# A hybrid decoder step: the level products of a gated recurrence, read with both heads' keys over all 128 rows

## The reference

```python
def step(S, inp):                      # 4 heads, dk = dv = 64
    qi, bi, ki, vi = inp               # bi: running sum of log forget gates
    diff = bi[:, :, :, None, :] - bi[:, :, None, :, :]
    decay = jnp.exp(jnp.where(causal[:, :, None], diff, NEG_BIG))
    att = jnp.einsum('bhtc,bhsc,bhtsc->bhts', qi, ki, decay)
    o = jnp.einsum('bhts,bhsv->bhtv', att, vi) + jnp.einsum('bhtc,bhcv->bhtv', qi * jnp.exp(bi), S)
```

## Time and profile before

| | us |
|---|---|
| median of 3 runs (827.66 to 829.39) | 829.32 |
| the profiled execution, time | 829.25 |
| its span, first to last instruction | 827.5 |
| PE busy | 816.1 (99%) |
| DVE busy | 570.0 (69%) |
| ACT busy | 436.8 (53%) |
| POOL busy | 264.2 (32%) |

### The profile page before, as it was taken

How to read it: one execution, slowest core, us unless ns; L and a number is a source line. 1 busy time by engine, 2 the same in 40 slices (tenths; PEclk the granted TensorE clock), 3 DMA queues, 4 the chain that set the end, 5 groups by cost and what they waited for, 6 DMA issues and landing times.

```text
span 827.5 us, 18120 instructions
## 1 busy us (share of the span) xinstructions
PE 816.1 (99%) x7016; PEld 801.4 (97%) x7016; DVE 570.0 (69%) x768; ACT 436.8 (53%) x621; POOL 264.2 (32%) x230
## 2 busy tenths in 40 slices
PE   9999999999999999999999999999999999999995
PEld 8999999999999999999999999999999999999995
DVE  7778787676877666554576688957787776645553
ACT  6553376645557665434353634774555666643442
POOL 4585282036710000121147825801565000001220
PEclk9999999999999999999999999999999999999999
DMA  9896859767657778776659968887665876776751
GB/s 314 235 319 256 301 162 324 237 227 269 218 179 253 240 241 306 248 262 226 205 164 247 312 234 278 241 259 256 232 237 179 260 247 221 260 280 234 250 203 52
DMA packets 171035, 200.00 MB, mean 242 GB/s; under 512 B 19680, under 2 KB 168496, under 8 KB 169648
## 3 DMA queue, kind: packets, MB, share of 16 engines
q1 hardware_dynamic: 169584, 197.02, 72.4%
q10 hardware_dynamic: 1392, 2.15, 0.7%
HBM read 191.25 MB, written 51.90 MB: 294 GB/s over the span
## 4 chain that ended last, share of the span: by engine, by line
PE 95%; DVE 3%; DMA 0%; ACT 0%; issue 0%; DVEq 0%; ACTq 0%
PE main L644 28%; PE main L645 28%; PE main L646 27%; PE small L694 2%; PE small L660 1%; PE small L646 1%; PE small L645 1%; PE small L644 1%; DVE w_lo L1189 1%; PE small L705 1%; DVE h_lo L1205 0%; DMA raw<-in_w_in 0%; PE small L798 0%; PE small L853 0%; PE small L722 0%; PE main L615 0%
## 5 line engine op out<-in xcount | busy, mean ns | idle before, releaser
L954 ACT ACTIVATE w_hi<-raw 128x1024 fp32r<-128x1024 f32 (+1 forms) x256 | 266.2, 1041 | 247.9 <-PE main L646 186.9
L1189 DVE TENSOR_TENSOR w_lo<-raw,w_hi 128x1024 fp32r<-128x1024 f32 (+1 forms) x256 | 337.3, 1318 | 64.6 <-ACT w_hi L954 60.6
L644 PE MATMUL main<-h_hi,w_hi 128*128 128x264 f32 x1264 | 365.6, 289 | 0.9 <-DVE w_lo L1189 0.8
L645 PE MATMUL main<-h_lo,w_hi 128*128 128x264 f32 x1264 | 358.8, 284 | 0.0
L646 PE MATMUL main<-h_hi,w_lo 128*128 128x264 f32 x1264 | 358.6, 284 | 0.0
L644 PEld LDWEIGHTS main<-h_hi,w_hi 128*128 128x128 f32 x1264 | 238.7, 189 | 5.9 <-DVE w_lo L1189 1.7
L645 PEld LDWEIGHTS main<-h_lo,w_hi 128*128 128x128 f32 x1264 | 239.0, 189 | 0.2
L646 PEld LDWEIGHTS main<-h_hi,w_lo 128*128 128x128 f32 x1264 | 237.6, 188 | 0.0
L644 PE MATMUL main<-a_hi,w_hi 128*128 128x264 f32 x512 | 145.3, 284 | 0.0
L645 PE MATMUL main<-a_lo,w_hi 128*128 128x264 f32 x512 | 145.0, 283 | 0.0
L646 PE MATMUL main<-a_hi,w_lo 128*128 128x264 f32 x512 | 145.0, 283 | 0.0
(11 more groups left out here) (222 smaller groups left out, 1030.0 us busy)
## 6 DMA issues: line engine op xcount, KB each, us to landing
raw<-in_w_in SPq DMA_DIRECT2D x48, 1024.0 KB, 5.8
raw<-in_w_up SPq DMA_DIRECT2D x32, 1024.0 KB, 5.3
raw<-in_w_down SPq DMA_DIRECT2D x32, 1024.0 KB, 5.2
out_kvs<-in_cache SPq DMA_DIRECT2D x48, 512.0 KB
out_kvs<-in_cache SPq DMA_DIRECT2D x32, 496.0 KB
raw<-in_w_o SPq DMA_DIRECT2D x8, 1024.0 KB, 5.3
raw<-in_w_br SPq DMA_DIRECT2D x8, 768.0 KB, 5.1
gates<-q_scratch SPq DMA_DIRECT2D x4, 768.0 KB, 7.2
```

Of the source, the lines that this page charges most:

```text
L644: pe.matmul(out[:, 0:TOK], wh, rh, start=start and k == 0, stop=False)
L645: pe.matmul(out[:, 0:TOK], wh, rl, start=False, stop=False)
L954: act.activation(w_hi[:, slot(l, u), 0:k, :], raw_of(u, k), ACT.Copy).then_inc(w_hi_ready, 1)
L1189: dve.tensor_tensor(w_lo[:, slot(l, u), 0:k, :], raw_of(u, k), w_hi[:, slot(l, u), 0:k, :].bitcast(F32), ALU.subtract).then_inc(w_lo_ready, 1)
```

## The change

- **Level products.** The queries are laid out in `q_bd` as head 0's rows with the rest zero, then head 1's rows with the rest zero (POOL clears it, ACT copies twice 64 rows, behind the `w_hi` split of unit 8, `q_bd_ready`). `q_lv` then holds both heads' padded late queries, so one matmul over 128 rows with 2 x 64 query columns serves both heads: 4 matmuls at levels 1 to 7 into one bank, 4 of 256 columns at level 0, 2 of 256 at level 8. Level 1 reads `kg` itself as its keys, so POOL makes no `k_lv` there. DVE's masked copies are one of 512 elements a level instead of two of 256.
- **Start of layer 0.** `unit_lo_last` also serves units 6 and 7; `w_lo` of unit 6 is made ahead of `bounds`, that of unit 7 behind it and ahead of the decays. ACT issues the first weight piece ahead of the small gain load.

```diff
@@ -73,7 +73,8 @@
 TURNS = (
     ["norm1"]
     + ["values T", "sample values T"]
-    + [f"level {i} {h}" for i in range(9) for h in range(2)]
+    + ["level 0 0", "level 0 1"]
+    + [f"level {i}" for i in range(1, 9)]
     + ["recurrence", "decayed keys T", "state"]
     + ["sample q T", "sample kv T 0", "sample kv T 1"]
     + ["scores 0 0", "scores 1 0", "scores 0 1", "scores 1 1", "scores 0 2", "scores 1 2"]
...
@@ -206,6 +207,10 @@
         swapped_qk = gates[:, 4:10, :]
         q_rows = gates[:, 12:24, :].rearrange("p a t -> p (a t)")[:, 0:SAMPLES * NG * P].rearrange(
             "p (b g c) -> p b g c", b=SAMPLES, g=NG)
+
+        q_bd = v_cache[:, :, :, :].rearrange("p b g c -> p (b g c)")[:, 0:4 * PROMPT].rearrange(
+            "p (h a t) -> p h a t", h=2, a=2)
+        final_k = q_lv[:, 1, :, :, :].rearrange("p h a c -> p (h a c)").rearrange("p (a t) -> p a t", a=2)
 
         ident = consts[:, K_ID:K_ID + P]
         ones = consts[:, K_ONE:K_ONE + P]
...
@@ -662,38 +668,31 @@
 
             def level(l, i):
 
-                if i:
-                    pe.wait_ge(level_ready, l * 8 + i)
-                else:
+                if i == 0:
                     pe.wait_ge(kg_ready, l + 1)
-                    z_ready(pe, l, CT_CQ + 1)
-
-                def operands(hp, h):
-                    rows = slice(h * HD, (h + 1) * HD)
-                    if i:
-                        return k_lv[rows, i % 2, hp, :], q_lv[rows, i % 2, hp, :]
-                    return kg[rows, hp, 0:PROMPT], z[rows, CT_CQ + hp, 0:PROMPT]
-
-                def queries(qq, tb):
-
-                    if not i:
-                        return qq[:, tb * P:tb * P + P]
-                    return qq[:, tb * P:tb * P + P].rearrange("p (n s t) -> p n s t", s=2, t=LEVELS[i - 1])[:, :, 1, :]
-                w = HALF if i else P
-                early = P - LEVELS[i - 1] if 0 < i < 8 else P
-                banks = [use_bank(pe, l, f"level {i} {h}") for h in range(2)]
+                    pe.wait_ge(q_bd_ready, l * 2 + 2)
+                    for hp in range(2):
+                        bank = use_bank(pe, l, f"level 0 {hp}")
+                        for tb in range(2):
+                            ts = slice(tb * P, tb * P + P)
+                            mm = pe.matmul(bank[:, tb * 2 * P:(tb + 1) * 2 * P], kg[:, hp, ts], q_bd[:, :, hp, ts],
+                                           start=True, stop=True)
+                        done(mm, f"level 0 {hp}")
+                    return
+                pe.wait_ge(level_ready, l * 8 + i)
+                bank = use_bank(pe, l, f"level {i}")
                 for hp in range(2):
-                    for tb in range(2 if i < 8 else 1):
-                        for h in range(2):
-                            kk, qq = operands(hp, h)
-                            if i == 8:
-                                out, kk, qq = banks[h][:, hp * P:hp * P + P], kk[:, 0:P], qq[:, P:2 * P]
-                            else:
-                                c = (hp * 2 + tb) * w
-                                out, kk, qq = banks[h][0:early, c:c + w], kk[:, tb * P:tb * P + early], queries(qq, tb)
-                            mm = pe.matmul(out, kk, qq, start=True, stop=True)
-                            if hp == 1 and (i == 8 or tb == 1):
-                                done(mm, f"level {i} {h}")
+                    if i == 8:
+                        mm = pe.matmul(bank[:, hp * 2 * P:(hp + 1) * 2 * P], k_lv[:, 0, hp, 0:P], q_lv[:, 0, :, hp, :],
+                                       start=True, stop=True)
+                        continue
+                    early = P - LEVELS[i - 1]
+                    for tb in range(2):
+                        keys = kg[:, hp, :] if i == 1 else k_lv[:, i % 2, hp, :]
+                        c = (hp * 2 + tb) * P
+                        mm = pe.matmul(bank[0:early, c:c + P], keys[:, tb * P:tb * P + early],
+                                       q_lv[:, i % 2, :, hp, tb * HALF:(tb + 1) * HALF], start=True, stop=True)
+                done(mm, f"level {i}")
 
             def scores(l, j, gs):
 
...
@@ -868,9 +867,10 @@
                 for u, (kind, n) in enumerate(UNIT_KINDS):
                     if l == 0 and u < 4:
                         continue
-                    if l == 0 and u < 6:
+                    if l == 0 and u < 8:
                         pe.wait_ge(out_taken, u + 1)
                         unit_lo_last(u, main[u % 4]).then_inc(w_used, 1)
+                        between(l, n)
                         continue
                     pe.wait_ge(w_lo_ready, l * UNITS + u + 5)
                     if kind == "in":
...
@@ -994,6 +994,13 @@
                     step(act.activation(kg[:, :, :], z[:, CT_CF:CT_CF + 2, :], ACT.Sigmoid, scale=-1.0))
                     act.activation(z[:, CT_CF:CT_CF + 2, :], z[:, CT_CF:CT_CF + 2, :], ACT.Sigmoid)\
                        .then_inc(sigmoids, 1)
+                if u == 5:
+                    z_ready(act, l, CT_CQ + 1)
+                    act.wait_ge(q_zeroed, l + 1)
+                    for h in range(2):
+                        rows = slice(h * HD, (h + 1) * HD)
+                        act.activation(q_bd[rows, h, :, :], z[rows, CT_CQ:CT_CQ + 2, 0:PROMPT], ACT.Copy)\
+                           .then_inc(q_bd_ready, 1)
                 if u == 8:
                     z_ready(act, l, CT_CO + 1)
                     act.activation(o_c[:, :, :], z[:, CT_CO:CT_CO + 2, :], ACT.Sigmoid).then_inc(sigmoids, 1)
...
@@ -1090,8 +1096,9 @@
             def square(k):
                 act.activation(square_of(k), x[:, k, :], ACT.Square).then_inc(squared, 1)
 
+            act.dma_start(piece_raw(0), piece_source(0)).then_inc(piece_landed[0], 16)
             act.dma_start(cur[:, C_G1:C_G1 + KT], io["gain0"]).then_inc(gain_in, 16)
-            for i in range(3):
+            for i in range(1, 3):
                 act.dma_start(piece_raw(i), piece_source(i)).then_inc(piece_landed[i], 16)
             act.wait_ge(setup_done, 1)
...
@@ -1269,23 +1276,24 @@
                     if i == 0:
                         dve.wait_ge(levels_in, 16)
                         dve.wait_ge(att_clear, l + 1)
-                    for h in range(2):
-                        name = f"level {i} {h}"
+                    for hp in range(1 if i else 2):
+                        name = f"level {i}" if i else f"level 0 {hp}"
                         bank = take(dve, l, name)
                         wait_ends(dve)
                         if i:
                             half = LEVELS[i - 1]
                             early, n, c = P - half, HALF // half, P + (i - 1) * HALF
-                            dst = att[0:early, h, :, :].rearrange("p a (n s t) -> p a n s t", s=2, t=half)[:, :, :, 1, :]
+                            dst = att[0:early, :, :, :].rearrange("p a h (n s t) -> p (a h) n s t", s=2, t=half)[:, :, :, 1, :]
                             mask = levels[0:early, c:c + HALF].rearrange("p (n t) -> p n t", n=n)
-                            src = bank[0:early, 0:4 * HALF].rearrange("p (a n t) -> p a n t", a=4, n=n)
-                            mask = mask.unsqueeze(1).to_broadcast([early, 4, n, half])
+                            src = bank[0:early, :].rearrange("p (a n t) -> p a n t", a=8, n=n)
+                            mask = mask.unsqueeze(1).to_broadcast([early, 8, n, half])
                         else:
-                            dst, mask = att[:, h, :, :], levels[:, 0:P].unsqueeze(1).to_broadcast([P, 4, P])
+                            dst = att[:, hp * 2:hp * 2 + 2, :, :].rearrange("p a h c -> p (a h) c")
+                            mask = levels[:, 0:P].unsqueeze(1).to_broadcast([P, 4, P])
                             src = bank[:, :].rearrange("p (a c) -> p a c", a=4)
                         ins = dve.copy_predicated(dst, mask.bitcast(U32), src)
                         ins.then_inc(masked, 1)
-                        dve.wait_ge(masked, l * 16 + 2 * i + h + 1)
+                        dve.wait_ge(masked, l * 9 + (i + 2 if i else hp + 1))
                         dve.sem_inc(bank_taken[TURN[name] % 4], 1)
 
                 def mask_scores(j):
...
@@ -1367,10 +1375,11 @@
                         dve.wait_ge(state_s_ready, l + 1)
                     evacuate(l, u)
                     if u == 3:
+                        split_lo(l, at + 3)
                         if l == 0:
                             bounds()
                             new_params()
-                        split_lo(l, at + 3)
+                            split_lo(l, at + 4)
 
                         dve.wait_ge(sigmoids, 2 * l + 1)
                         for hp in range(2):
...
@@ -1491,7 +1500,7 @@
                         dve.wait_ge(y_hi_ready, 3 * l + 3)
                         dve.tensor_tensor(y_lo[:, 0, :], y_a[:, :], y_hi[:, 0, :].bitcast(F32), ALU.subtract)\
                            .then_inc(y_ready, 1)
```

(20 more changed lines are left out.)

28 lines of the change are left out of this document (14 added, 14 removed).

## The result

| | before | changed |
|---|---|---|
| median of 4 runs each | 828.54 | 833.77 (832.98 to 834.67) |
| the profiled execution, time / span | 829.25 / 827.5 | 833.25 / 831.5 |

The ratio is 1.0064 (95% interval 1.0045 to 1.0082): slower, and 0.5 us above the forecast. Both kernels' times come in steps of 1.6 to 1.7 us (before: 827.7 or 829.3). A step is one drop of PE's granted clock to half for 3.41 us, told of at the end. The two profiled executions have one each and lie 4.0 us apart; the medians lie 5.2 apart, since the runs of the kernel before have none or one and those of the changed kernel one or two.

What follows compares the result with a forecast made beforehand. PE, busy 816.1 of 827.5 us, was taken to bound the kernel, with POOL feeding it. 829.25 + 1.65 (level 8) + 2.4 (unit 20) = 833.3; own range 831.2 to 835.5, 8 in 10 827.0 to 836.5.

Steps and rivals of the forecast that it cites:

- the two level terms: Start of level 8 in each layer: PE waits for POOL, +1.0 in layer 0 and +0.65 in layer 1.
- the unit 20 terms: Unit 20 in both layers: PE waits for a DVE split delayed by POOL's later work, +1.2 a layer, +2.4.
- Waits of units 6 and 7, -1.35: Start of layer 0: PE's two waits for `w_lo` go, saving 1.35 us.
- First weight piece earlier, -0.2: Start of layer 0: first weight piece lands up to 0.43 earlier, of which the ACT chain uses 0.2.
- PE's level stages: PE at levels: 0.87 each at levels 1 to 7, level 0 +0.6, level 8 unchanged; -1.1 a layer if PE sets pace.
- The query product, +0.69 a level: POOL at the levels: doubling to 512 elements adds 0.69 a product, making POOL's cycle 4.68 against PE's 3.78.
- Level 8, +1.0 in layer 0 and +0.65 in layer 1: POOL's operands come late, so PE starts level 8 at 67.7 in layer 0 and 472.1 in layer 1.
- The gains of start and PE are spent in this wait: Layer 0: POOL sets level 8's start, 1.0 later than before, so earlier savings at start and PE's levels are lost.
- Unit 20, +1.2 a layer: POOL work pushed behind level 8 locks out DVE's rotary products and splits; PE waits at unit 20, +2.4 in all.
- POOL keeps up: Rival at the levels: query product grows 0.3 or less or splits fit better, no level late; 825.5, chance 0.16.
- PE's stages get dearer: Rival at PE's levels: no edge saved, overlap of two heads' rows lost, +0.5 a layer; 833.8 or 828.7, chance 0.10.

Runs made afterwards that it cites:

- e3: Changed kernel with POOL's query product cut to 256 elements, head 1's half of the padded queries left zero; median 827.20, ratio 0.9988.
- e5: Changed kernel with gain load first and ACT copying the queries into the pads, POOL multiplying 256 elements a level; median 824.69, ratio 0.9960.
- e7: Changed kernel with gain load first and the start part undone, so the level products alone; median 834.81, ratio 1.0075.
- e1: Changed kernel with the small gain load issued ahead of the first weight piece again; median 832.53, ratio 1.0046.
- e4: Changed kernel with DVE's splits of units 19 and 20 moved ahead of its rotary products; median 828.78, ratio 1.0006.
- e6: e5 with e4's edit, the splits of units 19 and 20 ahead of the rotary products; median 824.67, ratio 0.9954.
- e11: Changed kernel with the one-column products divided, half of them moved behind unit 25; runs 831.53 to 832.00.
- e8: e6 with the one-column products divided, half of them moved behind unit 25; runs 825.24 to 825.65.
- e10: e7 with the one-column products divided, half of them moved behind unit 25; runs 831.79 to 832.50.
- e12: Changed kernel with gain load first, ACT making pads, level 0 unpadded, splits of units 19 and 20 before rotary products, one-column products divided; median 824.70, ratio 0.9958.

## Why the prediction was right, and where it was not

The sign, the total (833.3 for 833.77) and the mechanism hold: POOL's doubled query product makes PE wait at levels 6 to 8 and, through DVE, at unit 20; e3 removes the product's second half and both waits. That the total is as close as it is, is luck: errors of its terms cancel. Against the forecast the gain load adds 1.0 at level 8, the rest of the two level terms is 1.9 too large, and the unit 20 terms are 0.7 too small. The forecast start of level 8 in layer 1, 472.1, was met by chance too (472.37): the forecast had left layer 0's delay out of it, and the trace before has its drop of 1.65 ahead of that place, the changed kernel's behind it.

- *Waits of units 6 and 7, -1.35*: right. From unit 4 to unit 8 PE takes 14.00 instead of 14.94, with 0.35 to 0.45 more of level 0 in it: -1.3.
- *First weight piece earlier, -0.2*: wrong, +1.1. The forecast priced what moved forward and not what moved back: `h_hi` needs the gain, and its landing is what ACT waits for (1.46).
- *PE's level stages*: 0.88 against 0.87 at levels 1 to 6, right; level 7 1.22, mis-sized; level 0 +0.35 to +0.45 instead of +0.6. Together they are worth 0.9 to 1.0 a layer where POOL keeps up (e5), for -1.1.
- *The query product, +0.69 a level*: too much. By itself it takes 1.28 (e7, 41.07), 0.54 more than 0.74; and it now begins in time to meet the split itself, so that the key product no longer stands: cycle 4.43 at the last levels, not 4.68. Before that it isn't one number: the query products of levels 3 to 6 start 4.78, 5.38 and 4.61 apart.
- *Level 8, +1.0 in layer 0 and +0.65 in layer 1*: mis-sized. +0.57 (of which 1.03 is the gain load, by e1) and +0.21: 1.9 us less than forecast apart from the gain. How these 1.9 divide over the smaller product, DVE's splits and POOL's waits was not measured. "The gains of start and PE are spent in this wait" is false for the start: without it (e7) POOL's third level waits for PE's first, so most of the lead is kept, 1.64 of 2.20 at level 8 and 1.3 in the whole.
- *Unit 20, +1.2 a layer*: right in place and mechanism, too small. +1.60 and +1.50 from level 8 to unit 20. The sum counted POOL's added work and let 1.4 us of it fall into gaps. By DVE's starts in layer 0, the split of unit 20 starts 2.53 later (81.23 for 78.70): the chain behind unit 15 starts 0.3 later and saves 0.4 at the mask and 0.7 at the first rotary product, and it loses 1.0, 0.8 and 1.6 where the split of unit 18, the second rotary product and the split of unit 19 stand for POOL.

The rule of the Trainium skill that POOL and DVE lock each other out for a whole instruction (SBUF — State Buffer, "SBUF: two separate sides") carries this term. By that rule, the long durations shown here agree: 3.41 for a split of 1.22 that starts 2.3 us before a POOL product ends, 1.97 for one that starts 0.9 us before the end of a product of 1.52.

The rule of the Trainium skill that spoke against the change (TensorE: Matmul & The Clock Gate, "Part 3: Packing small matmuls — row/col tiling") holds for levels 0 and 7. At level 0, 8 products of 64 rows and 128 columns take 1.09 from their start to the next unit's, and 4 padded ones of 256 take 1.54; at level 7 it is 0.61 for eight and 1.02 for four padded. At level 2, where the weights are 126 columns wide and 64 columns move, the measurement decides against it (1.02 for eight in the earlier trace rows, 0.80 for four padded), and by the stages it does so at levels 1 to 6, least at level 6 (0.88 for 1.03).

Of the rivals, "POOL keeps up" is what e5 builds: 824.7 and, with one drop as in the profiled execution before, 826.4, 0.9 above its 825.5. "PE's stages get dearer" is refuted as a whole by e3 and e5; only levels 0 and 7 got dearer.

## What to carry to other kernels

A change that saves the bounding engine 1 us a layer (e5) can cost 1.9 (e7) if it hands its feeder half a microsecond a step: write the feeder's cycle beside the consumer's before padding anything for the consumer, and let an engine with idle time do the padding. Two engines that exclude each other turn work that is pushed later into waits of a third, so ask what stands behind the late work in every queue; putting a split that PE needs ahead of work that nobody awaits gave 3 us here while POOL was late (e4), and nothing once it was not (e6). And of two DMA issues that change places, price the one that moves back.

## What was not expected of the hardware

PE's clock falls in the middle of full work. In the changed kernel's trace, layer 1: the one-column products (32 matmuls, 64 records), then stretches before, in and after the drop (the third figure from the right is the granted clock; 1.00 is 2.4 GHz, 0.50 is 1.2 GHz), and the stretch in the same place of e11.

```profile
508.22 2.03 PE L797 MATMUL small<-z,state_s 64*64 64x1 f32 x64
```

```profile
508.00:511.00 3.00, 3.00 (x74) 2.84 (x73) 2.37 (x4) 1.18 (x2) 3.00 (x2) 1.00 1.10 329
511.10:514.50 3.40, 3.40 (x18) 3.40 (x18) 2.38 (x2) 0.38 (x1) 3.40 (x2) 0.50 0.10 28
514.60:518.00 3.40, 3.40 (x30) 3.40 (x29) 2.44 (x3) 2.60 (x3) 3.21 (x3) 1.00 0.95 299
```

```profile
509.10:512.50 3.40, 3.40 (x33) 3.26 (x32) 3.25 (x3) 0.60 (x1) 3.40 (x3) 1.00 0.53 159
```

Behind the 32 products PE runs at half clock for 3.41 us, from 511.13 on, and its matmuls come every 0.22 us instead of 0.12, in none, one or both layers of an execution, which makes the steps of 1.6 to 1.7 us. PE was busy throughout; what was unusual was that for 2 us it moved one column a matmul. Divided in two groups of 16, four kernels (e8, e10, e11, e12) show no drop: their four traces have none in the work, and the times of all 20 runs lie within 0.8 us of each other for each kernel. Undivided, all four runs of e7 had two and all four of the changed kernel one or two. The division is thus what removes the drop; which property of the 32 products brings it is not shown. Four transpositions stand behind them (from 510.18 on), and the division leaves these behind unit 24 with the first 16. Which executions of an undivided kernel drop was not settled either.

A load issued half a microsecond later behind a large one held its consumer up by 1.66 us (5.79 for 4.13), three times the delay of its issue. In e1 the consumer did not wait for it at all, so the landing itself moved by at least as much.
